# Expert tiles of a top-2 mixture: gate and up matmuls ahead of the second transposes, next rows copied ahead of the activation, down weights issued first

## The reference

```python
    a = jnp.einsum('td,edf->tef', t, w_gate)
    u = jnp.einsum('td,edf->tef', t, w_up)
    hid = jax.nn.silu(a) * u * gates.astype(t.dtype)[..., None]
    y = jnp.einsum('tef,efd->td', hid, w_down)
```

## Time and profile before

| | |
|---|---|
| Median of 3 runs | 1613.76 us (1613.31 to 1620.27) |
| The profiled execution's own time | 1615.13 us |
| Its span in the trace | 1613.4 us |
| TensorE busy | 1388.2 us, 86% |
| VectorE, ScalarE, GpSimd busy | 728.6, 434.2 and 245.3 us |
| Read and written | 244.43 MB and 37.29 MB |

### The profile page before, as it was taken

One profiled execution on the slowest core, in us unless ns is written; L12 is line 12 of the kernel. 1 busy time (PEld: TensorE's weight loads), 2 busy tenths in 40 slices (PEclk: granted clock), 3 DMA queues, 4 the chain that ended last, 5 costly groups with the idle time before them and its releaser, 6 DMA issues.

```text
span 1613.4 us, 22451 instructions
## 1 busy us (share of the span) xinstructions
PE 1388.2 (86%) x8194; PEld 840.4 (52%) x8194; DVE 728.6 (45%) x1673; ACT 434.2 (27%) x991; POOL 245.3 (15%) x374
## 2 busy tenths in 40 slices
PE   4999978999998699999479997799999939999950
PEld 3455455777676454545144554477776724454420
DVE  0345325767544334343345442377764343343426
ACT  2111146666301011111121103466660101111112
POOL 3311020000200122111302001100011010111114
PEclk8899989999998799999789997899999959999985
DMA  9500694001305699999560034800111029999943
GB/s 333 188 12 1 246 372 102 1 1 41 118 40 183 233 356 356 386 372 359 181 224 12 1 106 168 250 2 2 40 51 42 27 82 352 367 370 368 369 161 146
DMA packets 152035, 283.17 MB, mean 176 GB/s; under 512 B 7312, under 2 KB 95632, under 8 KB 146928
## 3 DMA queue, kind: packets, MB, share of 16 engines
q1 hardware_dynamic: 126832, 197.41, 36.5%
q0 software_dynamic: 25088, 84.24, 14.0%
HBM read 244.43 MB, written 37.29 MB: 175 GB/s over the span
## 4 chain that ended last, share of the span: by engine, by line
PE 50%; DVE 8%; DMA 5%; DVEq 2%; issue 2%; ACT 1%; POOL 0%; SPq 0%; POOLq 0%; ACTq 0%
PE ps L1903 16%; PE ps L1926 7%; PE ps L1642 7%; PE ps L1540 6%; PE ps L1818 4%; PE ps L1698 3%; PE ps L1751 2%; DMA ring<-in_w_mod 2%; DMA ring<-in_moe_w_up 1%; DVE ring L1221 1%; DVE x L1059 1%; DVEq L1053 1%; PE ps L1558 1%; PE ps L1874 1%; PE ps L1840 1%
## 5 line engine op out<-in xcount | busy, mean ns | idle before, releaser
L1903 PE MATMUL ps<-ring,hT_region 128*128 128x512 f32 x624 | 279.9, 602 | 2.6 <-DVE hT_region L1482 1.7
L1642 PE MATMUL ps<-ring,hT_region 128*128 128x512 f32 (+1 forms) x640 | 270.6, 579 | 1.7 <-ACT hT_region L848 1.7
L1221 DVE TENSOR_SCALAR_CACHE_REDUCE ring<-ps 128x768 f32<-128x768 f32 (+1 forms) x168 | 132.7, 820 | 164.8 <-PE ps L1698 108.4
L1642 PEld LDWEIGHTS ps<-ring,hT_region 128*128 128x128 f32 x640 | 121.2, 193 | 133.5 <-issue 132.7
L1903 PEld LDWEIGHTS ps<-ring,hT_region 128*128 128x128 f32 x624 | 117.6, 194 | 137.9 <-issue 137.0
L907 ACT ACTIVATE ring<-ring,negm 128x768 f32<-128x768 f32 (+1 forms) x168 | 137.7, 820 | 33.3 <-DVE ring L1221 33.2
L1818 PE MATMUL ps<-ring,hT_region 128*128 128x384 f32 (+1 forms) x480 | 141.8, 453 | 0.0
L1926 PE MATMUL ps<-arena,work 128*128 128x512 f32 x312 | 140.5, 593 | 1.1 <-DVE work L1505 1.1
L1698 PE MATMUL ps<-arena,qT 64*128 64x384 f32 (+1 forms) x640 | 127.5, 517 | 13.2 <-DVE ring L1221 5.7
L1489 DVE TENSOR_SCALAR work<-work 128x256 f32<-128x256 f32 x39 | 11.5, 294 | 263.2 <-ACT work L995 263.2
L1818 PEld LDWEIGHTS ps<-ring,hT_region 128*128 128x128 f32 x480 | 89.8, 190 | 44.2 <-issue 0.7
(11 more groups left out here) (270 smaller groups left out, 1612.0 us busy)
## 6 DMA issues: line engine op xcount, KB each, us to landing
ring<-in_w_mod SPq DMA_DIRECT2D x24, 2048.0 KB, 12.1
ring<-in_moe_w_gate SPq DMA_DIRECT2D x39, 1024.0 KB, 11.9
ring<-in_moe_w_up SPq DMA_DIRECT2D x39, 1024.0 KB, 15.4
arena<-in_moe_w_down SPq DMA_DIRECT2D x39, 1024.0 KB, 7.9
y_rows<-arena POOLq DMA_DIRECT2D x39, 512.0 KB, 7.7
ring<-in_w_in SPq DMA_DIRECT2D x6, 2048.0 KB, 18.9
y_rows<-x POOLq DMA_DIRECT2D x1, 7680.0 KB, 25.9
arena<-mod_rows POOLq DMA_DIRECT2D x14, 512.0 KB, 6.2
```

The lines of the kernel that those rows point to most:

```text
L1221: ts(o_, i_, -pair_of(p)[4], None, ALU.mult, ALU.min, accum_out=col).then_inc(m_ready, 1)
L1642: last = mm(ps[:, b, 0:n], hT[:, c, t * P:(t + 1) * P], w[:, c, :], start=(c == 0), stop=(c == KC - 1))
L1903: last = mm(ps[:, 2 + i % 2, :], hgT[i % 2][:, c, :], w[:, c, :], start=(c == 0), stop=(c == KC - 1))
```

## The change

Three edits of order, none of which adds or removes an operation:

- SyncE: for tile `i` the down weights of tile `i - 1` are issued before the gate and up weights of tile `i`, not behind them.
- VectorE: in turn `i`, `rows_in(i + 1)` stands before `hidden(i)`.
- TensorE: in turn `i`, `gate_up(i)` stands before `hidden_T(i - 1)`.

```diff
@@ sync
                 if kind == "moe":
+                    if i >= 1:
+                        down_weights(l, i - 1)
                     with if_used(sp, i):
                         slot_free(g)
...
                                          ).then_inc(wgu_landed[l][i % RING], 16)
-                    if i >= 1:
-                        down_weights(l, i - 1)
                     if i == N_ET - 1:
@@ vector
                         hiddenT(i - 1)
+                    if i + 1 < N_ET:
+                        rows_in(i + 1)
                     if i < N_ET:
                         hidden(i)
-                    if i + 1 < N_ET:
-                        rows_in(i + 1)
                     if i >= 1:
                         y_copy(i - 1)
@@ tensor
                 for i in range(N_ET + 1):
+                    if i < N_ET:
+                        gate_up(i)
                     if i >= 1:
                         hidden_T(i - 1)
-                    if i < N_ET:
-                        gate_up(i)
                     if i + 1 < N_ET:
                         rows_T(i + 1)
```

## The result

The changed kernel takes 1730.72 us in the median (1728.85 to 1745.04, 4 runs) where the one before takes 1614.34 (4 runs, one more than above): a ratio of 1.0732, interval 1.0669 to 1.0795. I forecast 1670 with a range up to 1698. The sign and the place were right; the loss is twice the forecast.

The account below looks back on a forecast made before the run. Steady tiles fill TensorE and DMA together, thanks to weights asked for early; the change halves that lead to 11.42 us. Layer 1 +26.2, layer 0 +28.9 and cover +1 make 56 us on 1615.13: 1671, median 1670, range 1638 to 1698.

Parts of the forecast that it names:

- what the text said they could: Compute edits at tile 1: gate and up could start 2.6 us earlier, but the late weights take this away.
- two chains: Tiles' loop: a tile starts 11.42 us after the last tile's start and c after tile i-2's end, at the earliest.
- One sign: SyncE's queue after the change: gate issued for the tile that starts next but one, 10 us ahead of its use.
- a rival at 15%: TensorE's clock falls in each stall: +27 us if all 16 did, about 1697; clock or contention in full, chance 0.15.
- the stalls of 3.1 us: Waits for weights in the tiles' loop: 3.08 us per pair, one stall at every other tile or two small ones.
- My price for one fall, 1.7 us: TensorE after 3.35 us of idle: mean granted clock 0.72 over 6 us, 1.7 us lost.
- The two rows: TensorE idles before the change: 3.35 us followed by a clock of 0.72, 2.73 us by none lost; a limit between.
- c: Time from the end of down matmuls until the pair issued behind them is usable: 14.5 us, kept at 13.0 to 16.0.
- The bound from below, 14.0: Lower bound on c: the measured 15.95 us contains about 2 us in which the batch before was still draining.
- The whole case, 15.95: Upper bound on c: layer 0, from tile 17's gate and up start at 746.49 to the up landing at 762.44.
- 49 for the pairs: Both layers' loops: 8 pairs of tiles in each, 3.08 us a pair, +24.6 us for each layer.
- 4 for small loads and the first tiles: Small loads in layer 0 +3 us, bounds 0 and +6; start of layer 1 +0.9, of layer 0 +1.6.

Follow-up runs that it names:

- the run with only the wait in front: Against the compute edits alone, SyncE's order of before: gate and up weights from tile 3 on wait for down matmuls of tile i-3; 1650.35 us, ratio 1.0221.
- the last run above: Against the changed kernel: down weights of odd tiles wait also until the same tile's gate and up weights have landed; 1719.73 us, one run.

## Why the prediction missed by half

**The mechanism held.** The pair behind the wait is the next tile's; its lead is 11.42 us; two chains interleave and the stall comes at every other tile. The compute edits gave what the text said they could, once the weights let them (2.5 and 2.7 us in the two layers, measured alone), and in the changed kernel the weights took it away: tile 1 of layer 1 starts 13.84 us after tile 0 and waits for its up weights. The down matmuls are not behind the row transposes (693.16 to 694.05 is 0.89). One sign was written down wrongly: the gate weights behind the wait are for the tile that starts next, 14.5 us after their issue (699.60 to 714.08), as the working itself has it, and not for the next but one 10 us ahead of its use.

**First wrong step: the clock, counted at nothing and kept as a rival at 15%.** I put the stalls of 3.1 us between an idle of 2.73 that kept the clock and one of 3.35 that lost it, and the sum has no term for a fall. The stalls in the loops came at 2.6 to 7.9 us of idle. The windows around 714.08 (after 5.00 us of idle):

```profile
711.00:713.00 2.00, 0.00 (x0) 0.00 (x0) 0.00 (x0) 0.00 (x0) 0.98 (x1) 0.99 1.11 380
713.00:719.00 6.00, 4.92 (x6) 2.18 (x7) 0.00 (x0) 0.00 (x0) 0.00 (x0) 0.50 1.01 369
719.00:721.00 2.00, 2.00 (x5) 0.84 (x4) 0.00 (x0) 0.00 (x0) 0.00 (x0) 0.80 1.09 367
```

Granted 1.00 up to 713, then 0.50, the lower of the two levels (1.2 GHz), until the engine had worked for some 5 us. Behind each of the 17 stalls in the two loops gate and up were slow: TensorE's busy time rose by 39 us, and filling the idle gave back 31. My price for one fall, 1.7 us, was low too: it is that of one row, in which the clock was 0.50 from 848 to 850 us and 1.00 again from 852. In the loops gate and up took 8.6 to 10.2 us for 7.03, so a fall cost 1.6 to 3.2 us, 2.4 in the mean; why some falls last longer, no run tests. The rival with its right price, 16 x 2.4 = 38, would have closed 38 of the 61 us between forecast and result.

The two rows were also read as if a length of idle decided. Two tiles of the changed kernel, the last of layer 0 and tile 1 of layer 1:

```profile
831.60 8.83 PE L1903 MATMUL ps<-ring,hT_region 128*128 128x512 f32 x16 [2.62 <-DMA ring<-in_moe_w_up]
...
1410.96 7.13 PE L1903 MATMUL ps<-ring,hT_region 128*128 128x512 f32 x16 [3.20 <-DMA ring<-in_moe_w_up]
```

An idle of 2.62 us lost the clock and one of 3.20 kept it. The run with only the wait in front has the same: 2.77 us ahead of slow matmuls (8.83 us), 3.28 ahead of fast ones (7.13). So stalls of 3.1 us could have gone either way, and a forecast that puts them at nothing needed luck. At 3.75 us and more every stall of the changed kernel lost it.

**Second: c, 14.5 us estimated, 15.8 the mean in layer 1 and 16.4 in layer 0.** The sum was 0.70 + 1.9 + 11.4 + 0.5. What stood between 698.40, the issue of the down weights, and the landing at 714.0:

```profile
697.00:698.00 1.00, 1.00 (x4) 0.46 (x3) 0.88 (x3) 0.31 (x1) 0.00 (x0) 1.00 0.00 0
...
699.00:700.00 1.00, 1.00 (x3) 0.38 (x2) 0.00 (x0) 0.00 (x0) 0.69 (x2) 1.00 1.20 123
700.00:701.00 1.00, 1.00 (x4) 0.46 (x3) 0.00 (x0) 0.00 (x0) 0.70 (x1) 1.00 0.47 131
701.00:702.00 1.00, 1.00 (x4) 0.49 (x3) 0.00 (x0) 0.00 (x0) 0.00 (x0) 1.00 1.01 360
702.00:703.00 1.00, 1.00 (x3) 0.38 (x2) 0.00 (x0) 0.00 (x0) 0.00 (x0) 1.00 0.92 254
703.00:704.00 1.00, 1.00 (x4) 0.45 (x3) 0.00 (x0) 0.00 (x0) 0.00 (x0) 1.00 0.89 348
704.00:705.00 1.00, 1.00 (x8) 0.77 (x7) 0.22 (x1) 0.39 (x1) 0.00 (x0) 1.00 1.01 404
...
711.00:712.00 1.00, 0.00 (x0) 0.00 (x0) 0.00 (x0) 0.00 (x0) 0.86 (x1) 1.00 1.27 389
```

The first issue comes 0.91 us behind the down matmuls, not 0.70. Traffic begins sooner than I took it (at 699), but creeps for five microseconds: 1.22 MB by 704. From then on it runs at some 350 to 404 GB/s. This batch is a long one, 15.68 us from its issue to the start. In layer 1, away from the small loads, c is 15.34 to 15.74 us six times of eight, about 1 us over the sum, and 16.51 and 16.65 twice. In layer 0 the tiles among the small loads have 17.38 and 19.52.

Where the 1 us lies, a batch that has the engines to itself tells, that of tile 9 in the last run above (issued at 1508.48, used at 1523.09):

```profile
1508.48:1514.40 5.92, 5.32 (x13) 2.46 (x14) 0.16 (x1) 0.00 (x0) 1.53 (x2) 1.00 0.80 228
1514.40:1521.60 7.20, 6.37 (x23) 3.16 (x21) 4.43 (x7) 1.58 (x3) 0.00 (x0) 1.00 1.07 375
1521.60:1522.60 1.00, 0.00 (x0) 0.00 (x0) 0.08 (x1) 0.00 (x0) 0.57 (x1) 1.00 0.47 148
1522.60:1523.09 0.49, 0.01 (x1) 0.01 (x1) 0.00 (x0) 0.00 (x0) 0.23 (x1) 1.00 0.00 0
```

The sum has 1.9 + 11.4 + 0.5 = 13.8 us from issue to use; here they are 14.61. The first 5.92 us bring 1.35 MB where 1.9 us of nothing and then 367 GB/s would have brought 1.48: 0.3 us. The middle runs at 375, a gain of 0.2. In the last microsecond of traffic the rate falls to 148: 0.6 us. The 0.5 for the tail, for which I had no row, came true: 0.49 us without traffic. With 0.2 for the later issue, this is the microsecond. So the mis-sized term is the batch, 1.9 + 11.4 = 13.3 us and measured 14.1: I took the mean rate of a full stream, in which the end of one batch lies beside the start of the next, for a batch that stands alone and runs out slowly.

The bound from below, 14.0, has the same fault: from the measured 15.95 I took off 2 us in which the batch before was draining, as if the new batch could have moved its bytes at full rate then. The whole case, 15.95, was the better estimate, though it was measured in a full stream and its nearness may be luck.

Waiting made 80 us (9 x 4.98 + 8 x 4.36, the mean excess over 11.42 in layers 0 and 1) where I had 49 for the pairs and 4 for small loads and the first tiles.

Together: 80 by waiting and 39 by the clock are 119, less 1.1 of stalls that the loops had before; measured in the loops, 117.4. What stays open is why a burst starts slowly (a long idle of the queues isn't needed for it, a queue that never empties wasn't tried), and why two of layer 1's eight batches take 1 us more than the others.

The Trainium skill's estimate (DMA: Bandwidth & Descriptors, Anatomy of one DMA), 2.0 us and 436 GB/s, gave c near 12.3. The Trainium skill states it there for one transfer that GpSimd issues; here five share the engines, three of them SyncE's weights, and the measured 15.8 shows that it doesn't carry over to such a batch. (With the other terms of my sum a c of 12.3 makes near 19 us, not the 15 that I wrote.) The Trainium skill's account of the clock (TensorE: Matmul & The Clock Gate, HAM oscillation), waits for data that send the matmuls behind them to half speed each time, is what the profile shows behind the 17 stalls of the loops, but not behind the 3.20 us ahead of tile 1.

## What to carry to other kernels

Before swapping two issues on one queue, name the wait that the first one carries and count, in tiles, how far ahead the second is then asked for: a wait in front shrinks the whole queue's lead to its own. A prefetch whose lead is about one period of the loop lies at the edge, because the slow start and the slow end of a batch, which lie beside other batches in a full stream, become bare there. And when a forecast has a TensorE stall near the lengths at which the clock was seen to fall (2.6 to 3.4 us gave both outcomes here), price both together, for each stall can cost two and a half microseconds more in slow matmuls.

## What the runs showed of the hardware

- Added TensorE work made the kernel faster: 28 transposes of the identity (3.22 us) in each stall took the median from 1731 to 1705 us.
- In layer 1 stalls of 3.8 to 5.1 us cost 1.6 to 3.1 us more in the gate and up matmuls behind them.
- An idle of 2.62 us lost the clock and one of 3.20 us kept it, in the same execution.
- One more store of 0.5 MB in each burst cost 2.2 us of waiting for each stall (1.9 in layer 1), where its bytes at 367 GB/s are 1.4.
- A batch of 4.19 MB alone on the engines took 14.61 us from its first issue to the matmuls that use it, where 4.19 MB in a full stream take 11.42.
- A copy from memory to memory of 2 MB showed as 656, 816, 0 and 852 GB/s in the four microseconds from 1452 us, 581 in the mean, above the 350 to 430 of the loads in the profile's count.
